# Conformer convolution: five taps of a unit by products and accumulating transfers instead of three, fewer diagonal taps, one closing sum in the second half

## What is computed

```python
def conformer_conv_module(h, w_pw1, b_pw1, w_dw, b_dw, ln_g, ln_b, w_pw2, b_pw2):
    u = h @ w_pw1 + b_pw1
    u = u[..., :CONV_CH] * jax.nn.sigmoid(u[..., CONV_CH:])
    u = causal_depthwise_conv(u, w_dw, b_dw)
    u = jax.nn.silu(layer_norm(u, ln_g, ln_b))
    return u @ w_pw2 + b_pw2
```

## Time and profile before

| | us |
|---|---|
| median of 3 runs | 2117.13 |
| lowest and highest run | 2114.44, 2119.14 |
| the profiled execution, its own time | 2112.95 |
| its span, first to last instruction | 2111.1 |
| the stretch of the 16 units, unit 0's first tap to unit 15's closing | about 1128 to 1448.5 |
| mean granted TensorE clock | 0.958 |

### The profile page before, as it was taken

The page is one execution under the profiler, slowest core; times in us unless marked ns, Lnnn a source line. Parts: engine busy times, 40 slices in busy tenths (PEclk is TensorE's granted clock), DMA queues, the critical chain, the costliest instruction groups (busy, mean ns, idle before and its releaser), DMA issues. The chain is left out here.

```text
span 2111.1 us, 47345 instructions
## 1 busy us (share of the span) xinstructions
PE 1917.9 (91%) x20718; PEld 1164.5 (55%) x20718; DVE 921.2 (44%) x1933; ACT 441.4 (21%) x994; POOL 441.4 (21%) x555
## 2 busy tenths in 40 slices
PE   7899999998699999989959999999969999898992
PEld 5666666665466655555644444445546665555651
DVE  2665565564721111111146999985172111111114
ACT  3332332234211111001133212223331111110110
POOL 2111110112123322222232111211222333221210
PEclk9999999999799999999989999999979999999996
DMA  9100000031699999999968552432179999999996
GB/s 313 31 1 1 1 0 0 0 120 61 253 400 417 428 422 426 423 427 424 407 231 216 117 107 67 93 76 95 44 303 413 416 425 422 426 425 425 424 382 250
DMA packets 101833, 523.23 MB, mean 248 GB/s; under 512 B 23382, under 2 KB 57226, under 8 KB 84224
## 3 DMA queue, kind: packets, MB, share of 16 engines
q1 hardware_dynamic: 74376, 463.00, 54.0%
q0 software_dynamic: 25504, 48.83, 8.4%
q10 hardware_dynamic: 1752, 8.44, 1.0%
HBM read 496.56 MB, written 34.65 MB: 252 GB/s over the span
## 5 line engine op out<-in xcount | busy, mean ns | idle before, releaser
L1349 PE MATMUL ps<-wgu,xT 128*32 128x256 f32 x7168 | 419.6, 387 | 35.4 <-issue 35.4
L1514 DVE TENSOR_TENSOR hh<-sg,ps 128x128 f32<-128x128 f32 x168 | 66.6, 396 | 704.8 <-ACT sg L1171 704.4
L1349 PEld LDWEIGHTS ps<-wgu,xT 128*32 128x32 f32 x7168 | 236.3, 112 | 195.3 <-issue 58.2
L1234 POOL DMA_INDIRECT y_rows<-my,yidx x168 | 166.8, 993 | 735.0 <-ACT my L1165 727.8
L2046 DVE SCALAR_TENSOR_TENSOR acc<-early_gu,par,acc 128x512 f32<-128x512 f32 x381 | 255.7, 743 | 0.0
L1349 PE MATMUL ps<-early_gu,xT 128*32 128x256 f32 x3584 | 213.6, 392 | 14.5 <-issue 11.9
L1364 PE MATMUL ps<-wd,hhT 128*32 128x256 f32 x3584 | 213.7, 379 | 0.0
L1171 ACT ACTIVATE sg<-ps 128x128 f32<-128x128 f32 x168 | 46.6, 278 | 685.3 <-PE ps L1349 685.3
L1349 PEld LDWEIGHTS ps<-early_gu,xT 128*32 128x32 f32 x3584 | 118.0, 113 | 97.8 <-issue 26.7
L1364 PEld LDWEIGHTS ps<-wd,hhT 128*32 128x32 f32 x3584 | 118.3, 110 | 75.1
L1777 PE MATMUL ps<-w_pw,c_hT 128*128 128x512 f32 x256 | 114.0, 600 | 6.6 <-ACT c_hT L1915 6.6
(11 more groups left out here) (341 smaller groups left out, 2120.0 us busy)
## 6 DMA issues: line engine op xcount, KB each, us to landing
wgu<-in_moe_w_gate_up SPq DMA_DIRECT2D x42, 4096.0 KB, 31.0
early_gu<-in_moe_w_gate_up SPq DMA_DIRECT2D x22, 4096.0 KB, 29.9
wd<-in_moe_w_down SPq DMA_DIRECT2D x42, 2048.0 KB, 29.3
early_wd<-in_moe_w_down SPq DMA_DIRECT2D x22, 2048.0 KB, 29.1
early_wd<-in_conv_w_pw SPq DMA_DIRECT2D x32, 512.0 KB, 5.4
conv<-prod POOLq DMA_DIRECT2D x42, 256.0 KB, 3.3
h_rows<-wgu ACTq DMA_DIRECT2D x8, 1024.0 KB, 4.2
early_gu<-in_w_in SPq DMA_DIRECT2D x2, 2048.0 KB, 16.8
```

The costliest lines, as they stand in the source:

```text
L1234: pool.indirect_dma_start(out=y_quarters, out_offset=bass.IndirectOffsetOnAxis(ap=yidx[:, tl, q:q + 1], axis=0), in_=y[:, n % YB, :], in_o ...
L1349: mm = pe.matmul(ps[TB * g:TB * g + TB, GU + n % 2, 0:2 * P].rearrange("p (a f) -> p a f", a=2), xT[:, q % 2, j, TB * tl:TB * tl + TB], wg ...
L1514: tt(hh[:, n % 2, :].rearrange("q (k f) -> q k f", k=KF), by_k(sg[:, n % 2, :]), by_k(ps[:, GU + n % 2, P:2 * P]), ALU.mult).then_inc(hh_r ...
```

## The change

The constants become 3 and 4 diagonal taps in the first half (added units, unit 7), 0 and 3 in the second (added units, unit 15), and 5 taps by transfers. A unit without diagonal taps skips TensorE's `convolve` and ScalarE's `spread_taps`, and VectorE closes it with one sum straight into `conv`. VectorE then has 23 taps in units 0 to 6, 27 in unit 7, 26 in units 8 to 14 and 28 in unit 15. The last `add_to_x` of unit 15 moves from tap 28 to tap 27, which is its last. The remaining lines count semaphores by the units that have diagonal taps.

```diff
-    PE_TAPS = (4, 2)
-    PE_TAPS_ADDED = (4, 1)
-    ADDED = 3
+    PE_TAPS = (4, 3)
+    PE_TAPS_ADDED = (3, 0)
+    ADDED = 5
...
-    steps_to = lambda unit: sum(dve_taps(n) + 1 for n in range(unit))
+    steps_to = lambda unit: sum(dve_taps(n) + (pe_taps(n) > 0) for n in range(unit))
+    with_diag = lambda unit: sum(pe_taps(n) > 0 for n in range(unit))
...
-            sp.wait_ge(pe_tapped, UNITS)
+            sp.wait_ge(pe_tapped, with_diag(UNITS))
...
             def convolve(unit):
+                if not pe_taps(unit):
+                    return
                 pe.wait_ge(gated, unit + 1)
-                pe.wait_ge(diag_ready, unit + 1)
+                pe.wait_ge(diag_ready, with_diag(unit) + 1)
...
             def spread_taps(unit):
+                if not pe_taps(unit):
+                    return
                 if unit >= 2:
-                    act.wait_ge(pe_tapped, unit - 1)
+                    act.wait_ge(pe_tapped, with_diag(unit - 1))
...
-            act.wait_ge(pe_tapped, UNITS)
+            act.wait_ge(pe_tapped, with_diag(UNITS))
...
-                      (15, 18): (3, 0), (15, 28): (3, 1)}
+                      (15, 18): (3, 0), (15, 27): (3, 1)}
...
                 dve.wait_ge(tapped, steps_to(unit) + dve_taps(unit))
+                if not pe_taps(unit):
+                    dve.tensor_tensor(conv[:, c, at0:at0 + HALF], acc[:, 0, :], acc[:, 1, :], ALU.add).then_inc(conv_ready, 1)
+                    return
                 dve.tensor_tensor(acc[:, 0, :], acc[:, 0, :], acc[:, 1, :], ALU.add).then_inc(tapped, 1)
-                dve.wait_ge(pe_tapped, unit + 1)
+                dve.wait_ge(pe_tapped, with_diag(unit + 1))
```

## The result

The changed kernel is slower. Over its own 6 runs and 6 of the kernel before, the ratio is 1.0078, 95% interval 1.0040 to 1.0116: 8 to 25 us more. A repetition on another occasion (12 runs against 35) gave 1.0056, interval 1.0017 to 1.0096. The medians were 2139.07 and 2116.06 us, the first outside the forecast's range.

What follows compares the result with a forecast made beforehand. VectorE and TensorE were taken as nearly full, with the added chain of transfers deciding. −0.2 us at unit 14's wait, −1.5 and −0.3 behind it sum to −2.0: 2111.0 us profiled, 2115.1 by the median; range 2106 to 2123.

Steps and rivals of the forecast that it cites:

- the second rival: Chain before `turn_conv(0)`: each load costs 3.3 us, the unit is 19.7, +8.8 us, 2125.9; chance 0.23.
- The likeliest forecast: Whole kernel: chain falls behind, unit 6 lands about 1279, `turn_conv(0)` starts at 1279.3 as before; −2.0 us, chance 0.55.
- The mechanism of the forecast: At `turn_conv(0)`: the chain falls behind, and both engines wait for unit 6's landing at 1279.2, first-half savings becoming a wait.
- the term for a load: Chain of transfers: each weight load delays it 2.1 us, bounded by 0 and 3.4, making its unit 18.0 us.
- The clock behind the wait: TensorE behind its 6.9 us idle at `turn_conv(0)`: a lower granted clock loses 2.4 us.
- The three waits for the SiLU: Turns 10, 12, 14, before `project_back`: removed tap saves nothing; 3.1 us idles could cost 3.4 us of clock, counted within the forecast.
- The odd turns: TensorE's turns 11, 13 and 15: a diagonal tap of 0.86 us falls away in each, 2.6 us saved.
- the four terms: Sum at VectorE's wait in unit 14: `turn_conv(0)` 0, clock +2.4, SiLU waits 0, odd turns −2.6; forecast −0.2 us.
- VectorE's savings: Units 0 to 6 save 4.7 us, units 8 to 14 10.2, unit 15 0.7; 15.6 if VectorE set the pace.
- The fast rival: Chain before `turn_conv(0)` keeps up: a load costs about 1 us, its unit is 16.7; −11.3 us, 2105.8; chance 0.22.

Runs made afterwards that it cites:

- half loads: Changed kernel with each weight load of units 2 to 15 cut to 4 of its 8 blocks; ratio 1.0283 to before, which can't be read; stretch 314.3 us.
- hardly any: Changed kernel with the weight loads of units 2 to 15 cut to 8 KB in place of 512; ratio 0.9981 to before.
- second half only: Kernel before with only the second half changed (units 8 to 14: 5 taps by transfers, none diagonal, one closing sum); ratio 0.9995 to before.
- unit 6 plain: Changed kernel with no transfers in unit 6 (4 diagonal taps, 27 on VectorE); ratio 0.9992 to before.
- four transfers: Changed kernel with four taps by transfers in all added units in place of five; ratio 1.0015 to before.

## Why the prediction was wrong

**Which way it went.** It came out as the second rival, "the chain falls further behind", which had 0.23 and +8.8 us; the profiled stretch gave +9.4 and +7.4. The likeliest forecast, −2.0, failed, and so did the range's upper end, 2123. The mechanism of the forecast, a chain that falls behind and a landing that holds both engines at `turn_conv(0)`, is what the runs show; how far it falls behind was off. That the rival's +8.8 is so near is luck in part: it put the landing 10.8 us late, where 8.3 were measured, and held nothing for the 3.5 us at the SiLU's waits below.

**The step that failed** is the term for a load: "I take 2.1, between the two that hit (1.2 and 3.4)". It measured 3.1, near the upper bound that I had given (2.7 by the weight loads themselves, the rest by the router's small loads, which the forecast left out). The rest of that part held: an undelayed unit of the chain 15.7 (a unit's first transfer, issued at about 1171.6 behind the last of the unit before, is followed 4.2 us later, at 1175.81; the others 3.55 apart), a load each 16.3 us, VectorE's unit 17.14 (17.13 forecast). With 3.1 in place of 2.1 the chain's unit is 19.4 and not 18.0. The landing came at 1288.8 and not at 1279.2: 7.1 us of the 9.6 by these five units, 0.5 by the last one, and 2.0 were there at unit 1's first transfer, 1.3 of them because the first gate itself came later. Against the first gate, `turn_conv(0)` moved by +8.3 where I had 0. The 2.1 came from two single hits, in a chain that mostly rested after a load; in the chain that is in flight all the time every one of the six loads hit, none for less than 1.9 us. The half loads cost 1.1 us at most.

**The clock behind the wait**: 2.4 forecast. `turn_conv(0)` took 1.94 in place of 1.03 and the gate's matmuls 8.59 in place of 7.03: 2.5 us.

**The three waits for the SiLU**: I named them and counted them as inside the forecast's spread. All three `project_back`s behind them ran at 8.80, where before one of three did: 3.5 us more, for a tap whose removal from there saved nothing, as forecast. This is the second size that was off: the forecast held 0, the trace of before had one of two idles of 2.23 us followed by a slow one, and the change made each 3.08.

**The odd turns** gave their 2.6 us. At VectorE's wait in unit 14 the sum of the four terms is then 8.3 + 2.5 + 3.5 − 2.6 = +11.7; measured from the first gates, 307.7 against 296.2, +11.5. Behind it −1.5 was right (unit 14 closed at +10.0), and unit 15 gave 0.6 in place of 0.3: +9.4.

**VectorE's savings** came as worked out up to unit 7 (4.9 against 4.7) and were all lost in its 12.10 us of idle, as the forecast's mechanism said.

**The rule of the Trainium skill.** The fast rival rested on a transfer losing no more than its packet time, 1.5 us, to a load. A load cost 3.1 on average and up to 7.67 − 3.55 = 4.1 for the transfer of 1175.81. The Trainium skill, "DMA: Bandwidth & Descriptors", section "SWDGE vs HWDGE vs iDMA", has an engine go round-robin between its queues. That each queue then gets an equal share of the time was my inference, which the section doesn't state; this case's transfers don't get it. Why is open: no run here separates the wait for the transfer's descriptors from that for its data.

## What to carry to other kernels

A chain of transfers that wait for one another is an engine of its own: compare its period, with the delays by all other traffic, with that of the work it runs beside, and look at what waits for its last member. A chain with little rest meets every load, so single hits on a chain that rests are too low a price. When two engines are near the bound, work taken from one is worth what the other's order allows. Here a few matmuls standing in a wait cost nothing and no half clock followed them, and independent work ordered into the waits was worth 3.5 and 4.3 us of the stretch, where taps removed from the odd turns gave 1.9.

## What was not expected of the hardware

- A chain of 256 KB accumulating transfers, each with 1.5 us of packets, lost 3.1 us on average for every two 512 KB loads (2.7 without the router's small ones) and 1.1 at most for every two of 256 KB.
- An idle of TensorE of 3.1 us between matmuls was followed by a `project_back` of 8.6 to 10.1 us in place of 7.03 in all 17 cases of seven profiles (the changed kernel twice, hardly any and half loads, second half only, unit 6 plain, four transfers), one of 2.2 us in 3 of 7, one of 1.35 in none of 6. The granted clock in the 10 us after the 15 us wait shows the same (window, columns as above):

```profile
1289.00:1299.00 10.00, 10.00 (x25) 5.20 (x24) 8.15 (x14) 1.45 (x2) 2.34 (x4) 0.77 0.01 2
```
